# The causal limit of stick breaking attention: a maximum and a product on VectorE in place of a matmul that adds to the scores

## The chip, the cores and the metric

The kernel runs on one core of one Trainium2 chip. The time is device microseconds of one execution of the whole program. A core has five engines with a queue each: TensorE (matmul, with its weight loads shown apart), VectorE, ScalarE, GpSimd and SyncE, which only issues transfers here. TensorE's clock has two levels, 1.2 and 2.4 GHz; the profile gives the granted clock as a share of the higher one.

## The reference

The program computes two transformer blocks on 1024 tokens of width 1024 in float32. The change lies in one stage of the first block, stick breaking attention with 8 heads of width 64:

```python
def stick_breaking_attention(q, k, v):        # per block of 128 queries, keys 0 to end
    z = jnp.einsum('bhqd,bhkd->bhqk', qb, kb).astype(jnp.float32) * scale
    mask = s_pos[None, :] < t_pos[:, None]
    log_one_minus = jnp.where(mask, jax.nn.log_sigmoid(-z), 0.0)
    shifted = jnp.concatenate(
        [log_one_minus[..., 1:], jnp.zeros_like(log_one_minus[..., :1])], axis=-1)
    between = lax.cumsum(shifted, axis=3, reverse=True)
    weights = jnp.where(mask, jnp.exp(jax.nn.log_sigmoid(z) + between), 0.0)
    outs.append(jnp.einsum('bhqk,bhkd->bhqd', weights.astype(vb.dtype), vb))
```

So the weight of key s for query t is sigmoid(z_ts) times the product of sigmoid(-z_tj) over all keys j between s and t, for s < t, and zero elsewhere. Only the 128x128 block on the diagonal holds both allowed and forbidden pairs; blocks beyond it are never computed.

## The kernel before

`stick_breaking` (from line 1693) runs some 300 us of the program, from about 240 to 542 us of the span. Its work is cut into N = 64 steps: step n is head n // 8 and query tile i = n % 8, with L = 128 (i + 1) keys, so the tiles of a head grow from 128x128 (step 0 of the head) to 128x1024 (step 7). What follows calls a step by its i. Beside the attention, the stage carries one projection (`lin_G`): each step also computes one tile of 128 tokens of one weight chunk, and each head one chunk, to fill TensorE.

No planner orders the work. `unrolled(N, [(lag, stage), ...])` writes each engine's queue out by hand: in turn m, an engine does each of its stages for step m - lag, in the order of the list. Engines meet through semaphores alone. Per step:

- TensorE: `scores` (lag 0, L1834 and L1836), `project_tile` (lag 4, L1867 and L1869), `turn_w`, the transposes of the weights (lag 2, L1844), and `values` (lag 3, L1854). The scores are products of q in two parts with k's high part and then k's low part, in pieces of 512 keys. At their end one more product adds `unit` x `limit`, both 128x128 in bf16, to the diagonal block: unit is the identity, limit is 0 for s < t and -1e30 elsewhere, so both sigmoids of a forbidden pair come out as 1 and 0.
- ScalarE: `sigmoids` writes sigmoid(-z) to sb_rest (L1891) once the scores are there, and sigmoid(z) to sb_wgt (L1894) once `turn_w` of two steps ago has read that buffer; then it copies the transposed weights to sb_wT (L1901, lag 2). In step 5 it also rounds q and k of the next head (L1882, L1883), and once per head the weight chunk (L405).
- VectorE: `stage_lin` (lag 4: L1937 and L1939, both from PSUM), `products` (a backward running product over sb_rest, L1919, then sb_wgt times sb_rest shifted by one key, L1922), and `output` (lag 3, the copy of the values to sb_o, L1930). In this order in every step. The scan works in place.
- GpSimd: the low parts, by a subtraction of rounded from full values: q (L1790) and k (L1794) of the next head, once ScalarE has rounded them, and the weight chunk in four pieces (L1814).

Three waits matter: `stage_lin` waits for the projection of its step; `values` of a step waits for `output` of the step before it (`reached(pe, out, n)`), since both use one PSUM bank; `output` sits behind `products` of a step three later in VectorE's queue. Buffers sb_rest, sb_wgt and sb_wT are double.

Of the kernel before, what the change touches and what calls it, by code (L numbers as in the profile page):

```python
# [19 lines left out]
BF = mybir.dt.bfloat16  # L20
# [4 lines left out]
P = 128  # L25
# [5 lines left out]
NEG = -1e30  # L31
# [1661 lines left out]
def stick_breaking(k, qkT, v, mix, lin, lin_dst, mod_stored):  # L1693
# [9 lines left out]
    with ExitStack() as c:  # L1703
        sem = lambda n: k.sem("sb_" + n)
        q = k.sb(c, "sb_q", [P, S])
        q_split = [k.sb(c, f"sb_q_split{s}", [P, S], R) for s in range(2)]
        kk, k_lo = [], []
        for s in range(2):
# [7 lines left out]
        wgt = [k.sb(c, f"sb_wgt{s}", [P, S]) for s in range(2)]  # L1716
        wT = [k.sb(c, f"sb_wT{s}", [P, NT, P]) for s in range(2)]
        o = [k.over(f"sb_o{s}", [P, NT, HD], F, k.w_hl_offset(s, 0, KT * LW)) for s in range(2)]
        limit = k.sb(c, "sb_limit", [P, P], BF)
        unit = k.sb(c, "sb_unit", [P, P], BF)  # L1720
        stage = [k.over(f"sb_stage{s}", [P, NT // 2, LW], F, k.w_hl_offset(s, 1, KT * LW)) for s in range(2)]
        lin_stored = [sem(f"lin_stored{s}") for s in range(2)]
        hi_lo = sem("hi_lo")
# [1 line left out]
        loaded = [sem(f"loaded{s}") for s in range(2)]  # L1725
        v_in = [sem(f"v_in{s}") for s in range(2)]
        stored = [sem(f"stored{s}") for s in range(2)]
        z_done, rest_done, beta_done, scanned, w_done, turned, wT_done, pv, out, his, los = (
            sem(n) for n in ("z", "rest", "beta", "scanned", "w", "turned", "wT", "pv", "out", "his", "los"))
        N = SB_HEADS * NT  # L1730
# [4 lines left out]
        with nc.Block() as block:  # L1735
# [46 lines left out]
            @block.gpsimd  # L1782
            def _(pool):
                def split_qk(n):
                    h, s = n // NT, n // NT % 2
                    if n % NT == 0:
                        pool.wait_ge(his, 2 * h + 1)
                        if h:
                            pool.wait_ge(*lin.at("w_ready", slot(h - 1), (h - 1) // 2 + 1))
                        pool.tensor_tensor(q_split[s][HD:P, :], q[HD:P, :], q_split[s][HD:P, :].bitcast(F),  # L1790
                                           ALU.subtract).then_inc(los, 1)
                        pool.wait_ge(los, 2 * h + 1)
                        pool.wait_ge(his, 2 * h + 2)
                        pool.tensor_tensor(k_lo[s][:, :], kk[s][:, :], k_hi[s][:, :].bitcast(F),  # L1794
                                           ALU.subtract).then_inc(los, 1)
                pool.memset(limit[:, :], 0.0).then_inc(made, 1)
                pool.memset(unit[:, :], 0.0).then_inc(made, 1)
                for s in range(2):
                    pool.memset(rest[s][:, :], 1.0).then_inc(made, 1)
                pool.wait_ge(made, 4)  # L1800
                pool.affine_select(out=limit[:, :], in_=limit[:, :], compare_op=ALU.is_gt, fill=NEG, base=0,
                                   pattern=[[-1, P]], channel_multiplier=1).then_inc(made, 1)
                pool.affine_select(out=unit[:, :], in_=unit[:, :], compare_op=ALU.not_equal, fill=1.0, base=0,
                                   pattern=[[-1, P]], channel_multiplier=1).then_inc(made, 1)
                pool.wait_ge(made, 6)
                split_qk(0)

                def split_lo(n):
                    part, sl, j = n % NT, slot(n // NT), n // NT // 2
                    if part < 4:  # L1810
                        if part == 0:
                            pool.wait_ge(*lin.at("w_hi_done", sl, j + 1))
                        cols = slice(part * KT * LW // 4, (part + 1) * KT * LW // 4)
                        lo = pool.tensor_tensor(k.w_lo[sl][:, cols], k.w_raw[sl][:, cols],  # L1814
                                                k.w_hi[sl][:, cols].bitcast(F), ALU.subtract)
                        if part == 3:
                            lo.then_inc(k.wsem["w_ready"][sl], 1)
                unrolled(N, [(0, split_lo), (-3, lambda n: split_qk(n) if n else None)])

            @block.tensor  # L1820
            def _(pe):
                pe.wait_ge(made, 6)

                def scores(n):
                    h, i = n // NT, n % NT
                    s, L = h % 2, (i + 1) * P
                    if i == 0:
                        pe.wait_ge(los, 2 * h + 2)
                        pe.wait_ge(loaded[s], 64 * (h // 2 + 1))
                    reached(pe, beta_done, n - 1)  # L1830
                    for a in range(0, L, 512):
                        b = min(L, a + 512)
                        for part in (k_hi, k_lo):
                            pe.matmul(zs(n, a, b), q_split[s][:, i * P:(i + 1) * P], part[s][:, a:b],  # L1834
                                      start=part is k_hi, stop=part is k_lo and b < L)
                    pe.matmul(zs(n, L - P, L), unit[:, :], limit[:, :], start=False, stop=True)\  # L1836
                      .then_inc(z_done, 1)

                def turn_w(n):
                    i = n % NT  # L1840
# [71 lines left out]
            @block.vector  # L1912
            def _(dve):
                def products(n):
                    L = (n % NT + 1) * P
                    w, left = wgt[n % 2], rest[n % 2]
                    dve.wait_ge(rest_done, n + 1)
                    back = left[:, 0:L][:, ::-1]
                    dve.tensor_tensor_scan(back, back, back, 1.0, ALU.mult, ALU.min).then_inc(scanned, 1)  # L1919
                    dve.wait_ge(scanned, n + 1)  # L1920
                    dve.wait_ge(beta_done, n + 1)
                    dve.tensor_tensor(w[:, 0:L], w[:, 0:L], left[:, 1:L + 1], ALU.mult).then_inc(w_done, 1)  # L1922

                def output(n):
                    h, i = n // NT, n % NT
                    s = h % 2
                    dve.wait_ge(pv, n + 1)
                    if i == 0:
                        reached(dve, stored[s], 16 * (h // 2))
                    dve.tensor_copy(o[s][:, i, :], k.bank[6][:, 0:HD]).then_inc(out, 1)  # L1930

                def stage_lin(n):
                    tile, sl, half = n % NT, slot(n // NT), n % NT // 4
                    dve.wait_ge(*lin.at("lin_mm", sl, NT * (n // NT // 2) + tile + 1))
                    if tile % 4 == 0:
                        reached(dve, lin_stored[half], 16 * (n // NT))
                    dve.tensor_copy(stage[half][:, tile % 4, :], k.bank[7][:, LW:2 * LW]).then_inc(hi_lo, 1)  # L1937
                    dve.wait_ge(hi_lo, n + 1)
                    dve.tensor_tensor(stage[half][:, tile % 4, :], k.bank[7][:, 0:LW], stage[half][:, tile % 4, :],  # L1939
                                      ALU.add).then_inc(k.wsem["lin_evac"][sl], 1)  # L1940
                unrolled(N, [(LATE, stage_lin), (0, products), (3, output)])


# [1637 lines left out]
```

## Time and profile before

| | us |
|---|---|
| three executions | 3300.24, 3302.2, 3306.65 (median 3302.2) |
| the profiled execution | 3302.0 |
| its span | 3300.3 |
| busy in the span: TensorE / weight loads | 2938.9 / 2526.1 |
| busy in the span: VectorE / ScalarE / GpSimd | 1851.4 / 1027.9 / 908.1 |
| busy from 243 to 540 us (297 us): TensorE / weight loads | 284.81 / 270.99 |
| busy from 243 to 540 us: VectorE / ScalarE / GpSimd | 205.94 / 138.72 / 88.43 |
| mean granted clock, whole span / 243 to 540 us | 0.943 / 0.95 |

The span is what the profiler saw; the time of an execution has a little around it. Busy times of engines overlap. The start of a matmul is recorded, its end is modelled, so the distance from one start to the next tells more than its duration. "Idle before" is the time in which an engine had nothing running ahead of an instruction, with the instruction that ended it.

### The profile page before, as it was taken

The page shows a single profiled execution, that of the slowest core. Times are in us where ns is not written, and L with a number is a line of the kernel's source. Part 1 is how long each engine was busy: PE and PEld are TensorE (multiplying, and loading weights), DVE is VectorE, ACT ScalarE, POOL GpSimd, SP SyncE. Part 2 cuts the span into 40 slices and gives each one's busy share as a digit, 9 for nine tenths or more (in the row PEclk, how much of TensorE's full clock was granted, in tenths as well). Part 3 has the DMA queues.
Part 4 walks back from the last instruction along what each step waited for, and adds up shares of the span by engine and source line. Part 5 has one row for each costly group of instructions (what it writes and reads, how often), then busy time and mean ns, then how long its engine had stood idle before and what let it go on. Part 6 is the DMA issues. An engine that isn't in the chain of part 4 may idle for free. (4 is left out here: it accounts for less than half of the span.)

```text
span 3300.3 us, 40638 instructions
## 1 busy us (share of the span) xinstructions
PE 2938.9 (89%) x15957; PEld 2526.1 (77%) x15957; DVE 1851.4 (56%) x2924; ACT 1027.9 (31%) x1466; POOL 908.1 (28%) x304
## 2 busy tenths in 40 slices
PE   4969998799999999979677678889999899999996
PEld 3869897687888888867556676789779688888885
DVE  7617764665454545562589877865336533333336
ACT  5424544222222222231456455633222111111111
POOL 1212331113233233340122512211121233333333
PEclk9989998799999999989788789999999999999998
DMA  6733333401111111101223322230102111111111
GB/s 225 264 103 72 72 76 125 164 16 72 40 50 46 56 51 38 64 26 62 67 83 124 92 63 60 63 116 28 43 20 71 64 51 41 48 51 51 51 51 51
DMA packets 112339, 240.06 MB, mean 73 GB/s; under 512 B 53524, under 2 KB 72471, under 8 KB 99015
## 3 DMA queue, kind: packets, MB, share of 16 engines
q1 hardware_dynamic: 107175, 220.70, 20.6%
q10 hardware_dynamic: 4320, 14.29, 1.3%
q0 software_dynamic: 704, 3.15, 0.3%
q8 instruction: 95, 1.56, 0.2%
q14 instruction: 45, 0.37, 0.0%
HBM read 202.58 MB, written 38.67 MB: 73 GB/s over the span
## 5 line engine op out<-in xcount | busy, mean ns | idle before, releaser
L1020 PE MATMUL psum<-h_hi,w_hl 128*128 128x512 f32 x2432 | 751.3, 390 | 16.8 <-DVE ffn_relu L1597 12.8
L1009 POOL TENSOR_TENSOR w_hl<-w_raw,w_hl 128x2048 fp32r<-128x2048 f32 x65 | 324.0, 4984 | 862.9 <-ACT w_hl L1003 862.9
L1020 PEld LDWEIGHTS psum<-h_hi,w_hl 128*128 128x128 f32 x2432 | 456.7, 188 | 113.7 <-issue 18.4
L1037 PE MATMUL psum<-w_hl,ffn_a_hi 128*128 128x512 f32 x1600 | 494.1, 390 | 6.5 <-DVE residual L1360 6.5
L1020 PE MATMUL psum<-h_lo,w_hl 128*128 128x512 f32 x1216 | 473.8, 390 | 0.0
L450 PE MATMUL psum<-w_hl,h_hi 128*128 128x256 f32 (+1 forms) x1920 | 353.8, 287 | 29.9 <-POOL w_hl L413 15.1
L1037 PEld LDWEIGHTS psum<-w_hl,ffn_a_hi 128*128 128x128 f32 x1600 | 301.3, 188 | 69.5 <-DVE residual L1360 6.9
L1003 ACT ACTIVATE w_hl<-w_raw 128x2048 fp32r<-128x2048 f32 x65 | 124.6, 1916 | 692.4 <-PE psum L1037 355.0
L413 POOL TENSOR_TENSOR w_hl<-w_raw,w_hl 128x2048 fp32r<-128x2048 f32 (+1 forms) x39 | 181.8, 4662 | 552.6 <-ACT w_hl L405 552.6
L450 PEld LDWEIGHTS psum<-w_hl,h_hi 128*128 128x128 f32 x1920 | 305.3, 196 | 31.7 <-issue 16.0
L1037 PE MATMUL psum<-w_hl,ffn_a_lo 128*128 128x512 f32 x800 | 311.9, 390 | 0.0
L450 PE MATMUL psum<-h_hi,w_hl 128*128 128x512 f32 (+1 forms) x864 | 254.8, 380 | 39.9 <-POOL h_lo L2855 19.8
L450 PE MATMUL psum<-w_hl,h_lo 128*128 128x256 f32 (+1 forms) x960 | 274.5, 286 | 0.0
L1360 DVE TENSOR_TENSOR residual<-residual,psum 128x512 f32<-128x512 f32 x176 | 120.2, 687 | 274.7 <-PE psum L1037 274.6
L1020 PEld LDWEIGHTS psum<-h_lo,w_hl 128*128 128x128 f32 x1216 | 228.7, 188 | 47.8
L1606 DVE TENSOR_TENSOR residual<-residual,psum 128x512 f32<-128x512 f32 x256 | 172.7, 685 | 132.3 <-PE psum L1037 132.2
L450 PEld LDWEIGHTS psum<-h_hi,w_hl 128*128 128x128 f32 x864 | 160.3, 192 | 71.0 <-POOL h_lo L2855 20.2
L1597 DVE TENSOR_SCALAR ffn_relu<-psum,ffn_b_up 128x512 f32<-128x512 f32 x64 | 46.5, 748 | 284.6 <-POOL ffn_a_lo L1571 158.3
L450 PEld LDWEIGHTS psum<-w_hl,h_lo 128*128 128x128 f32 x960 | 187.9, 196 | 0.0
L1347 DVE SCALAR_TENSOR_TENSOR ffn_u<-ffn_raw,ffn_conv,ffn_u 128x1024 f32<-128x1024 f32 x88 | 181.0, 2118 | 0.0
L1037 PEld LDWEIGHTS psum<-w_hl,ffn_a_lo 128*128 128x128 f32 x800 | 150.6, 188 | 31.4
L450 PE MATMUL psum<-h_lo,w_hl 128*128 128x512 f32 (+1 forms) x432 | 163.0, 377 | 0.0
(375 smaller groups left out, 5078.7 us busy)
## 6 DMA issues: line engine op xcount, KB each, us to landing
w_raw<-in_w_up SPq DMA_DIRECT2D x38, 1024.0 KB, 4.8
w_raw<-in_w_down SPq DMA_DIRECT2D x27, 1024.0 KB, 4.9
ada_w<-in_w_ada ACTq DMA_DIRECT2D x26, 512.0 KB, 4.6
w_raw<-in_w_in_T SPq DMA_DIRECT2D x12, 1024.0 KB, 7.0
ada_w<-in_w_ada SPq DMA_DIRECT2D x22, 512.0 KB, 5.3
w_raw<-in_xa_wkv SPq DMA_DIRECT2D x8, 1024.0 KB, 5.4
w_raw<-in_w_in_G SPq DMA_DIRECT2D x8, 648.0 KB, 5.4
p1G<-sb_stage SPq DMA_DIRECT2D x16, 324.0 KB, 3.6
```

Source lines behind the costliest of these rows:

```text
L413: pool.tensor_tensor(self.k.w_lo[s][:, 0:n], self.k.w_raw[s][:, 0:n], self.k.w_hi[s][:, 0:n].bitcast(F), ALU.subtract)\
L450: mm = pe.matmul(out, lhs, rhs, start=t == 0 and p == 0, stop=t == KT - 1 and p == 2)
L1003: act.activation(self.k.w_hi[s][:, :], self.k.w_raw[s][:, :], ACT.Copy)\
L1009: pool.tensor_tensor(self.k.w_lo[s][:, :], self.k.w_raw[s][:, :], self.k.w_hi[s][:, :].bitcast(F), ALU.subtract).then_inc(self.k.wsem["w_r ...
L1020: m = pe.matmul(k.bank[b][:, :], w[:, t * CW + f * P:t * CW + (f + 1) * P], h[:, t, half * 512:half * 512 + 512], start=t == 0 and w is w_ ...
L1037: m = pe.matmul(k.bank[4 + out % 4][:, :], a[f][:, tile * P:(tile + 1) * P], w[:, f * D + half * 512:f * D + half * 512 + 512], start=f == ...
L1347: dve.scalar_tensor_tensor(out=u[s][:, v, :], in0=raw[s][:, v, j:j + S], scalar=co, in1=u[s][:, v, :], op0=ALU.mult, op1=ALU.add)\
L1360: dve.tensor_tensor(k.x[:, tile, cols], k.x[:, tile, cols], k.bank[4 + o % 4][:, :], ALU.add)\
L1597: dve.tensor_scalar(r[:, b % 2, (b // 2) * 512:(b // 2) * 512 + 512], k.bank[b][:, :], bu[:, ds(2 * g + b % 2, 1)], 0.0, ALU.add, ALU.max) ...
L1606: dve.tensor_tensor(xt, xt, k.bank[4 + o % 4][:, :], ALU.add).then_inc(dn_out, 1)
```

## The change

The matmul with the limit goes. The constants `limit` and `unit` are replaced by `later` (1 for s >= t, 0 elsewhere) and `sooner` (1 for s < t, 0 elsewhere), both 128x128 in float32. In each step VectorE takes the maximum of `later` and the diagonal block of sb_rest before the scan, and multiplies the diagonal block of sb_wgt by `sooner` before the large product. Two semaphores order this. The wait for the constants moves from TensorE to VectorE; ScalarE keeps its own.

```diff
-        limit = k.sb(c, "sb_limit", [P, P], BF)
-        unit = k.sb(c, "sb_unit", [P, P], BF)
+        later = k.sb(c, "sb_later", [P, P])
+        sooner = k.sb(c, "sb_sooner", [P, P])
...
+        limited, weighed = sem("limited"), sem("weighed")
...
-                pool.memset(limit[:, :], 0.0).then_inc(made, 1)
-                pool.memset(unit[:, :], 0.0).then_inc(made, 1)
+                pool.memset(later[:, :], 0.0).then_inc(made, 1)
+                pool.memset(sooner[:, :], 1.0).then_inc(made, 1)
...
-                pool.affine_select(out=limit[:, :], in_=limit[:, :], compare_op=ALU.is_gt, fill=NEG, base=0,
+                pool.affine_select(out=later[:, :], in_=later[:, :], compare_op=ALU.is_gt, fill=1.0, base=0,
                                    pattern=[[-1, P]], channel_multiplier=1).then_inc(made, 1)
-                pool.affine_select(out=unit[:, :], in_=unit[:, :], compare_op=ALU.not_equal, fill=1.0, base=0,
+                pool.affine_select(out=sooner[:, :], in_=sooner[:, :], compare_op=ALU.is_gt, fill=0.0, base=0,
                                    pattern=[[-1, P]], channel_multiplier=1).then_inc(made, 1)
...
-                pe.wait_ge(made, 6)
-
                 def scores(n):
...
                         for part in (k_hi, k_lo):
-                            pe.matmul(zs(n, a, b), q_split[s][:, i * P:(i + 1) * P], part[s][:, a:b],
-                                      start=part is k_hi, stop=part is k_lo and b < L)
-                    pe.matmul(zs(n, L - P, L), unit[:, :], limit[:, :], start=False, stop=True)\
-                      .then_inc(z_done, 1)
+                            mm = pe.matmul(zs(n, a, b), q_split[s][:, i * P:(i + 1) * P], part[s][:, a:b],
+                                           start=part is k_hi, stop=part is k_lo)
+                    mm.then_inc(z_done, 1)
...
                     dve.wait_ge(rest_done, n + 1)
+                    dve.tensor_tensor(left[:, L - P:L], left[:, L - P:L], later[:, :], ALU.max).then_inc(limited, 1)
+                    dve.wait_ge(limited, n + 1)
                     back = left[:, 0:L][:, ::-1]
                     dve.tensor_tensor_scan(back, back, back, 1.0, ALU.mult, ALU.min).then_inc(scanned, 1)
+                    dve.wait_ge(beta_done, n + 1)
+                    dve.tensor_tensor(w[:, L - P:L], w[:, L - P:L], sooner[:, :], ALU.mult).then_inc(weighed, 1)
                     dve.wait_ge(scanned, n + 1)
-                    dve.wait_ge(beta_done, n + 1)
+                    dve.wait_ge(weighed, n + 1)
                     dve.tensor_tensor(w[:, 0:L], w[:, 0:L], left[:, 1:L + 1], ALU.mult).then_inc(w_done, 1)
...
+                dve.wait_ge(made, 6)
                 unrolled(N, [(LATE, stage_lin), (0, products), (3, output)])
```

## Rows read from the trace of the kernel before

**Rows 1.** Head by head: stretch, busy of PE, PEld, DVE, ACT, POOL, PEclk, DMA.

```profile
268.73:304.77 36.04, 34.29 (x270) 32.56 (x270) 26.13 (x41) 17.71 (x28) 12.35 (x6) 1.00 0.34 82
...
414.53:452.82 38.29, 36.74 (x271) 35.22 (x270) 25.29 (x41) 17.43 (x27) 11.97 (x6) 0.92 0.32 75
```

**Rows 2.** Waits of the whole stage: us in total, times, longest us.

```profile
PE psum L1854 <- DVE sb_o L1930: 11.7, 11, 1.6
...
DVE sb_stage L1937 <- PE psum L1869: 73.6, 51, 3.0
...
PEld psum L1836 <- issue: 7.4, 32, 0.5
...
PE psum L1844 <- DVE sb_wgt L1922: 0.5, 2, 0.3
```

**Rows 3.** TensorE's timeline at three head changes: start, duration, engine, line, operation [idle before].

```profile
374.51 0.82 PE L1844 MATMUL psum<-ident,sb_wgt 128*128 128x128 f32 x6
...
376.88 1.30 PE L1854 MATMUL psum<-w_raw,sb_wT 128*128 128x64 f32 x10 [1.55 <-DVE sb_o L1930]
...
381.56 0.52 PE L1854 MATMUL psum<-w_raw,sb_wT 128*128 128x64 f32 x3 [0.19 <-DVE sb_o L1930]
...
412.93 0.29 PE L1854 MATMUL psum<-w_raw,sb_wT 128*128 128x64 f32 x1 [1.55 <-DVE sb_o L1930]
...
420.43 0.33 PE L1854 MATMUL psum<-w_raw,sb_wT 128*128 128x64 f32 x2
```

**Rows 4.** VectorE's timeline, steps 5 to 7 of head 3, same columns.

```profile
366.03 0.33 DVE L1937 COPY sb_stage<-psum 128x162 f32<-128x162 f32 x1 [0.58 <-PE psum L1869]
...
366.64 1.75 DVE L1919 TENSOR_TENSOR_SCAN sb_rest<-sb_rest 128x768 f32<-128x768 f32 x1
...
368.42 0.96 DVE L1922 TENSOR_TENSOR sb_wgt<-sb_wgt,sb_rest 128x768 f32<-128x768 f32 x1
...
369.29 0.22 DVE L1930 COPY sb_o<-psum 128x64 f32<-128x64 f32 x1
...
370.76 2.73 DVE L1919 TENSOR_TENSOR_SCAN sb_rest<-sb_rest 128x896 f32<-128x896 f32 x1
...
373.52 3.08 DVE L1922 TENSOR_TENSOR sb_wgt<-sb_wgt,sb_rest 128x896 f32<-128x896 f32 x1
...
377.25 2.28 DVE L1919 TENSOR_TENSOR_SCAN sb_rest<-sb_rest 128x1024 f32<-128x1024 f32 x1
...
379.56 1.72 DVE L1922 TENSOR_TENSOR sb_wgt<-sb_wgt,sb_rest 128x1024 f32<-128x1024 f32 x1
```

**Rows 5.** GpSimd's timeline, the same stretch.

```profile
368.79 2.81 POOL L1790 TENSOR_TENSOR sb_q_split<-sb_q,sb_q_split 64x1024 fp32r<-64x1024 f32 x1 [22.17 <-ACT sb_q_split L1882]
...
371.69 3.97 POOL L1794 TENSOR_TENSOR sb_k_lo<-sb_k,sb_k_hi 128x1024 fp32r<-128x1024 f32 x1
...
378.34 5.55 POOL L1814 TENSOR_TENSOR w_hl<-w_raw,w_hl 128x324 fp32r<-128x324 f32 x4 [2.69 <-ACT w_hl L405]
```

**Rows 6.** GpSimd's timeline at the start of the stage.

```profile
237.31 2.35 POOL L1790 TENSOR_TENSOR sb_q_split<-sb_q,sb_q_split 64x1024 fp32r<-64x1024 f32 x1 [5.36 <-ACT sb_q_split L1882]
```

**Rows 7.** TensorE's timeline around one limit product.

```profile
367.58 0.34 PE L1834 MATMUL psum<-sb_k_lo,sb_q_split 128*128 128x384 f32 x1
...
367.76 0.23 PE L1836 MATMUL psum<-sb_limit,sb_unit 128*128 128x128 bf16 x1
...
367.80 0.40 PE L1867 MATMUL psum<-w_hl,h_hi 128*128 128x324 f32 x1
```

**Rows 8.** Two lines asked for: durations ns min/median/max of all their instructions.

```profile
L1922 DVE TENSOR_TENSOR sb_wgt<-sb_wgt,sb_rest x64: 292/802/3084, 244.0 to 527.3; 128x128 f32<-128x128 f32 x8, 128x256 f32<-128x256 f32 x8, 128x384 f32<-128x384 f32 x8, 128x512 f32<-128x512 f32 x8
...
L1814 POOL TENSOR_TENSOR w_hl<-w_raw,w_hl x32: 867/1031/1863, 242.0 to 493.7; 128x324 fp32r<-128x324 f32 x32
```

**Rows 9.** Two projections, columns as in rows 1.

```profile
378.29:380.44 2.15, 2.15 (x19) 2.15 (x18) 2.12 (x2) 0.28 (x1) 2.10 (x2) 1.00 1.01 292
...
415.09:419.02 3.93, 3.93 (x18) 3.93 (x18) 2.33 (x3) 0.28 (x1) 3.93 (x4) 0.50 0.60 193
```

## The prediction

> **What bounds the kernel now.** I first cut the stage by heads, from the start of one head's first score product to the next [rows 1]. Two of the six periods are 36.04 us at clock 1.00, the other four are longer at a lower mean clock, up to 38.29. In the 36.04 us TensorE is busy for 34.29 and VectorE for 26.13. So TensorE sets the pace, and the mean says that VectorE has 10 us free. The mean misleads: 1.75 us of TensorE's idle time per head has to be found. The list of waits [rows 2] says that TensorE's value products (L1854) waited 11 times, 11.7 us in all, for VectorE's copy to sb_o (L1930), while VectorE waited 73.6 us for the projection (L1869). VectorE has slack in some steps and is late in others. TensorE's timeline shows where: 1.55 us ahead of the value products of step 7, and 0.19 us ahead of those of step 0 of the next head [rows 3]. Nothing else in a full-clock head stops TensorE.
>
> Next I read why VectorE is late there, on VectorE's and GpSimd's timelines of the same 20 us [rows 4, 5]. The scan takes 1.75 us for 768 columns and 2.28 for 1024, so 2.01 would fit 896, but it took 2.73; the product took 0.29 for 128 [rows 8] and 0.96 for 768, so 1.09 would fit 896 and 1.22 fit 1024, but they took 3.08 and 1.72. GpSimd's q and k subtractions took 2.81 and 3.97 there against 2.35 for q's before VectorE had begun [rows 6] (k's is as wide, and I take 2.34). The sums agree with taking turns: the scan issued at 370.76 ends 1.9 us after q's subtraction (ended 371.60), k's subtraction then loses 1.63, and the product issued at 373.52 ends 0.94 us after k's ended at 375.66. So VectorE's work on two SBUF operands and GpSimd's subtractions exclude each other, and whoever waits gets the next turn. The copies and sums from PSUM (L1937, L1939) keep 0.33 us beside them.
> The Trainium skill (SBUF — State Buffer, § SBUF: two separate sides) states it as a lock held for the whole instruction, against a VectorE operation with two SBUF inputs; this speaks against a change that adds two such operations per step. Priced by their own durations alone they give the first rival below; priced by the lock, the forecast. By that rule, the trace agrees.
>
> **The change, part by part.**
> *Limit product removed (L1836), 64 times.* From its start to the next product is 0.04 us (367.76 to 367.80); from k_lo's product to the projection 0.22, of which its own 384 columns at 2.4 GHz are 0.16, which leaves 0.06 [rows 7]. I take 0.05 us each. The upper bound is 7.4 us of weight-load idle time "issue" before it in 32 cases [rows 2], 0.12 us each over 64. In the steps where TensorE waits for VectorE nothing is gained; some 43 steps are left (1 to 5 of seven heads, all of the last): a gain of 2.2 us, between 1.7 and 5.2.
> *Added:* maximum (sb_later) ahead of the scan and product (sb_sooner) after it, 64 times each, 128x128. The shortest product, on a 128x128 tile, took 292 ns [rows 8]. An operation waiting for the one before starts 0.03 us after its end (scan to product, 368.39 to 368.42), one that does not starts 0.08 before it (copy at 369.29, product end 369.38) [rows 4]. So the maximum costs 0.32, the second product 0.21: 0.53 us per step. Queued behind them on VectorE are the large product, the output copy and the next step's staging; TensorE waits for the copy (L1854), ScalarE for the large product.
> *Moved:* the wait for the constants goes from TensorE, which has its score products behind it, to VectorE, which has its staging and scans behind it; the constants, now float32, are still two memsets and two selects of GpSimd, which then idles 5.36 us for q's rounding [rows 6], and no score or sigmoid exists before this: nothing. ScalarE's first sigmoid may start 0.2 us sooner; VectorE starts on staging, not on it: nothing.
> *Steps 0 to 4:* VectorE idles before the next staging; the least of these times is 0.58 us (366.03, [rows 4]), their mean 73.6/51 = 1.4 us [rows 2]. It covers 0.53 in each.
> *Steps 5 to 0, walked on the full-clock head of rows 3 to 5.* In step 5 staging starts at 366.03, maximum 366.64, scan 366.96 to 368.71, small product to 368.92. Q's subtraction asks at 368.79, so it gets the next turn: to 371.27. The large product follows, to 372.2, copy to 372.3, and the values of step 6 start at 372.45, some 2 us late. Step 6: staging 372.2; k's subtraction has the turn from 372.15 to 374.5, then maximum to 374.8, scan to 376.8, small product to 377.0, large one to 378.15, copy to 378.3, values of step 7 at 378.4 instead of 376.88: **1.5 us late**. If q's subtraction comes after step 5's product, the waits change places but their sum is the same within 0.1.
> Step 7: TensorE, held up at step 6, ends its projection at 376.45 instead of 374.51; GpSimd's weight pieces started 3.83 us after this (378.34), so now at 380.3. Maximum from 378.75, scan 379.07 to 381.35. If a piece (0.87 us alone, rows 8) gets in before the small product and another before the large one, the values of step 0 start at 384.8; if the small product keeps the turn, at 383.9. Before: 381.56. So **2.3 to 3.25 us per head**, middle 2.8, at full clock.
> *The clock.* The 16 products of a projection took 2.15 us at clock 1.00 and 3.93 at 0.50, that is at 2.4 and at 1.2 GHz [rows 9], the slow one right after a stall of 1.55 us (412.93, [rows 3]). From the stalled values of step 7 to those of step 0 took 7.50 us there (412.93 to 420.43), against 4.68 [rows 3]. Three of the seven head changes lose a projection's clock like this; the same stall of 1.55 us left it at 1.00 in the others. With three stalls of 1 to 2 us in place of one I expect the clock to fall in three of the four heads that keep it now. There step 0's values come at 378.4 + 7.5 = 385.9, 4.3 us later than now. In the three that lose it now TensorE hides VectorE's step 7, and 1.55 us stay.
> *Start.* In head 0, TensorE already waits for VectorE's product (L1844) [rows 2], so the first steps' additions show: two steps of 0.53 and half a GpSimd piece, 1.5 us (0.5 to 3).
> *The sum:* 4 heads x (3/4 x 4.3 + 1/4 x 2.8) = 15.7; 3 x 1.55 = 4.7; start 1.5; product -2.2. Together +19.7. The profiled execution took 3302.0 us (span 3300.3 and 1.7 around it), the median of the three runs is 3302.2. 3302.0 + 19.7 = 3321.7, rounded to **3322**. Nothing after the stage is touched; it moves as a whole.
>
> **The rivals.**
> *A: VectorE pays only durations.* GpSimd's subtractions fall where the small operations are not hurt. Then steps 6 and 7 cost 0.53 each and another 0.2 of displaced idle time: 1.3 us x 7 = 9, start 1, product -2.2: 3310. For it: the total of GpSimd work is unchanged. Against: in steps 5 to 7 every turn is already contested [rows 4, 5].
> *B: slower still.* The three stalls keep the clock low twice per head. A second slow projection costs 1.8 us more [rows 9]: 7 x (4.3 + 1.8) = 43, less what is lost now in three heads (5.9, see C), start 1.5, product -2: 3339. For it: the stalls at steps 6, 7 and 0 lie 4 to 6 us apart. Against: a slow TensorE waits less, which ends the stalls.
> *C: faster.* The stall of step 7 goes with the low clock in three heads, at up to 2.25 us each (38.29 less 36.04, [rows 1]), 5.9 in all as an estimate. If the operations go one to a gap, the stall grows by 0.53 per head and its later place keeps the clock full: 3.7 + 0.5 - 5.9 - 5.2 (upper bound of the product) = -6.9: 3295. It decides from the point where the clock stays at 1.0 through all head changes. Against: more idle time of TensorE has gone with a lower clock in this trace, not a higher.
> *D: no change that can be told.* The additions sit in the stall as in A and the limit product gives its upper bound: 3302 + 9 + 0.5 - 5.2 = 3306.
>
> **How the numbers follow.** Forecast 0.55 (3313 to 3332), A 0.18, B 0.12, C 0.04, D 0.11. A measurement of this kernel tells 0.2%, 6.6 us. Faster is C: 0.04. Same is D and the lower part of A (below 3308.6): 0.15. Slower 0.81. The range leaves out C, half of D and half of B: 3305 to 3339.
>
> **What would show it.** In the profile after: L1836 gone and score to projection 0.17 us; two groups of 64 on VectorE, with a mean above 0.4 us because some waited for a turn, and a bare minimum of 0.29; values of L1854 waiting for L1930 now also at step 6, with 11.7 us grown to over 30; head periods of 38.3 to 40.5 us instead of 36.04; low clock at nearly every head change; q's subtraction at about 2.4 us since it starts first. I am wrong if the small operations show 0.29 us throughout (A), if idle time of L1854 does not grow, or if the clock stays at 1.0.

## The result: 0.13% slower, where 0.6% was forecast

The changed kernel took 3307.32 us in the median of 20 executions, the kernel before 3304.59 in 20 on the same chip; the ratio is 1.0013 with a 95% interval of 1.0007 to 1.0019, so 2 to 6 us more. The direction was right and the range held the time, but the forecast was +20 us and the measured difference is +4.3. Most of the expected loss did not come. One execution of the changed kernel, in its second series, took 9669.9 us and is left out of every number here; why is not known.

The page of the changed kernel (span 3302.3 us) shows the work moved as described: VectorE has 40 us more than the 1851.4 of before and 128 instructions more, TensorE 64 products fewer.

```profile
PE 2940.6 (89%) x15893; PEld 2530.5 (77%) x15893; DVE 1891.3 (57%) x3052; ACT 1027.1 (31%) x1466; POOL 892.4 (27%) x304
```

Two heads of the changed kernel, in the columns of [rows 1]:

```profile
309.84:346.89 37.05, 35.10 (x262) 33.81 (x262) 31.27 (x57) 17.59 (x28) 9.92 (x6) 0.95 0.35 80
...
457.75:497.68 39.93, 36.73 (x262) 35.45 (x262) 31.40 (x57) 16.31 (x26) 10.61 (x6) 0.91 0.32 74
```

Of its six head periods four are 36.77 to 37.05 us and two 39.9; the latter are called the dear heads below. The kernel before had 36.04 to 38.29, 36.73 in the mean; here the mean is 37.96. The stage (to the end of the last staging) ended at 547.5 us against 541.5. The two waits of [rows 2] in the stage, with their new line numbers (L1852 waits for L1932, L1939 for L1867):

```profile
PE psum L1852 <- DVE sb_o L1932: 16.9, 16, 1.7
...
DVE sb_stage L1939 <- PE psum L1867: 39.0, 24, 3.1
```

TensorE waited 16.9 us for VectorE's output copy instead of 11.7, not the 30 that I expected, and VectorE's waiting for the projection halved. The two new operations, grouped by form (count, busy us, mean ns of one, idle before):

```profile
L1916 DVE TENSOR_TENSOR sb_rest<-sb_rest,sb_later 128x128 f32<-128x128 f32 x64 | 28.5, 445 | 19.7 <-ACT sb_rest L1889 19.7
...
L1921 DVE TENSOR_TENSOR sb_wgt<-sb_wgt,sb_sooner 128x128 f32<-128x128 f32 x64 | 22.1, 345 | 0.0
```

VectorE's timeline in steps 5 to 7 of head 3, the lines that answer to [rows 4], and GpSimd's for [rows 5]:

```profile
373.08 0.27 DVE L1921 TENSOR_TENSOR sb_wgt<-sb_wgt,sb_sooner 128x128 f32<-128x128 f32 x1
...
373.45 2.98 DVE L1924 TENSOR_TENSOR sb_wgt<-sb_wgt,sb_rest 128x768 f32<-128x768 f32 x1
...
377.08 1.73 DVE L1916 TENSOR_TENSOR sb_rest<-sb_rest,sb_later 128x128 f32<-128x128 f32 x1
...
378.85 2.02 DVE L1919 TENSOR_TENSOR_SCAN sb_rest<-sb_rest 128x896 f32<-128x896 f32 x1
...
385.94 1.23 DVE L1924 TENSOR_TENSOR sb_wgt<-sb_wgt,sb_rest 128x1024 f32<-128x1024 f32 x1
```

```profile
373.25 2.37 POOL L1791 TENSOR_TENSOR sb_q_split<-sb_q,sb_q_split 64x1024 fp32r<-64x1024 f32 x1 [19.62 <-ACT sb_q_split L1880]
...
375.70 2.96 POOL L1795 TENSOR_TENSOR sb_k_lo<-sb_k,sb_k_hi 128x1024 fp32r<-128x1024 f32 x1
...
386.08 2.74 POOL L1815 TENSOR_TENSOR w_hl<-w_raw,w_hl 128x324 fp32r<-128x324 f32 x2 [7.42 <-ACT w_hl L405]
```

The large product of step 5 now takes 2.98 us instead of 0.96: q's subtraction (asked at 373.25) got its turn between the small product (ended 373.35) and it. The maximum of step 6 waited for k's subtraction (1.73 us), the scan over 896 columns then ran beside no subtraction (2.02 instead of 2.73), and the weight pieces came at 386.08, after step 7's large product had been issued (1.23 instead of 1.72). TensorE's timeline of the same head: three rows of step 6's scores and projection for [rows 7], and the value products in the turn of step 6 (they belong to the tile three steps earlier, by their lag of 3; start, duration, line, idle before):

```profile
372.04 0.34 PE L1833 MATMUL psum<-sb_k_lo,sb_q_split 128*128 128x384 f32 x1
...
372.22 0.31 PE L1865 MATMUL psum<-w_hl,h_hi 128*128 128x324 f32 x1
...
372.37 0.24 PE L1867 MATMUL psum<-w_hl,h_lo 128*128 128x162 f32 x1
...
376.72 0.52 PE L1852 MATMUL psum<-w_raw,sb_wT 128*128 128x64 f32 x3 [1.72 <-DVE sb_o L1932]
```

A new stall of 1.72 us stands at step 6. After it the clock fell, here in step 7. The rows below are step 7's scores and projection together, its projection alone (3.22 us at a mean clock of 0.61), and the start of its value products, which waited for nothing:

```profile
377.61:382.25 4.64, 4.64 (x23) 4.35 (x23) 4.50 (x5) 1.03 (x1) 1.05 (x1) 0.63 0.00 0
...
379.03:382.25 3.22, 3.22 (x18) 3.22 (x17) 3.12 (x4) 1.03 (x1) 0.00 (x0) 0.61 0.00 0
...
382.90 0.33 PE L1852 MATMUL psum<-w_raw,sb_wT 128*128 128x64 f32 x2
```

### The profile page after: what moved, and what is told of

Read it like the earlier page. It is cut to its first block and busy times, and to the rows that moved or that the text cites. A ratio compares the mean times of both kernels' runs of the same rounds, so it can differ in the third digit from the quotient of the medians.

```text
span 3302.3 us, 40638 instructions
## 1 busy us (share of the span) xinstructions
PE 2940.6 (89%) x15893; PEld 2530.5 (77%) x15893; DVE 1891.3 (57%) x3052; ACT 1027.1 (31%) x1466; POOL 892.4 (27%) x304
```

## The experiments

Theory after the result: (1) VectorE's work on two SBUF operands and GpSimd's subtractions take turns, and this, not the 0.53 us of the additions, sets what the change costs; (2) the limit product was dearer than I had it; (3) where the clock falls matters more than that it falls. Rivals are named with each run. Each ratio is against the kernel before on the same chip, medians in us. Periods are from the start of one head's first score product to the next.

### The limit product alone

```diff
...
-                    pe.matmul(zs(n, L - P, L), unit[:, :], limit[:, :], start=False, stop=True)\
-                      .then_inc(z_done, 1)
+                    mm.then_inc(z_done, 1)
```

> Before with the limit product L1836 left out and nothing in its place (the causal limit inside the diagonal blocks is not computed). Theory: the product costs TensorE 0.13 us per step, 0.04 until the next product starts and 0.09 that the next products start later, in every step in which TensorE does not wait. So score products plus projection take 2.60 us in step 3 instead of 2.74, a full-clock head 35.3 to 35.5 us instead of 36.04, the program 5 to 8 us less. Rival (the term of my prediction, 0.05 us): 2.69 us in step 3, a head 35.8 us, the program 2 to 3 us less.

Measured: 3297.13, ratio 0.9973 (0.9961 to 0.9984), 9 us less. Scores plus projection of step 3 take 2.60 us instead of 2.74, and a head at full clock:

```profile
305.19:340.65 35.46, 33.37 (x262) 32.42 (x262) 26.27 (x41) 17.69 (x28) 12.61 (x6) 1.00 0.35 83
```

35.46 us, as the theory has it; four of the six periods hold some low clock, at 36.5 to 36.6. The stage ends 6.7 us sooner than in the first profile of before and 3.2 sooner than in the second (below). The product is worth 0.13 us a step. The rows of [rows 7] show what I missed. Before, the first projection product stood 0.24 us ahead of the second (367.80 to 368.04, the next row of that timeline); now it is 0.15 (372.22 to 372.37). So the bf16 product cost 0.04 us until the next start and 0.09 after it.

### The additions alone

```diff
+                    dve.tensor_tensor(left[:, L - P:L], left[:, L - P:L], later[:, :], ALU.max).then_inc(limited, 1)
...
+                    dve.tensor_tensor(w[:, L - P:L], w[:, L - P:L], sooner[:, :], ALU.mult).then_inc(weighed, 1)
...
                     pe.matmul(zs(n, L - P, L), unit[:, :], limit[:, :], start=False, stop=True)\
                       .then_inc(z_done, 1)
```

> Before with the maximum and the small product added on VectorE and the limit product kept (the result stays the reference's). Theory: the additions alone cost what the change costs plus what the limit product gives back: head periods 37.5 to 37.8 us against 37.05 in the changed kernel, the program 9 to 12 us above before. Rival (limit product worth 0.05 us a step): 6 to 7 us above before. My prediction's price for the additions was 22 us.

Measured: 3311.27, ratio 1.0022 (1.0012 to 1.0033), 7 us more. Its stage ended 8.1 us later than in the first profile of before.

```profile
308.22:345.89 37.67, 35.93 (x270) 33.79 (x270) 31.33 (x57) 17.59 (x28) 9.91 (x6) 0.95 0.33 78
```

Four periods are 37.67 to 37.75, 0.63 above the changed kernel's 37.05, which is five unstalled steps at 0.13. The total came out below what I gave the theory and within its interval also where the rival stood, so this run alone doesn't decide between them; the periods do. What it settles is the price of the additions: 7 to 8 us, a third of the 22 that my sum had. The two parts do not add up to the whole: 9 us less and 7 us more would make the changed kernel 2 us faster, and it is 4 slower. The intervals of the two (5 to 13 us less, 4 to 11 more) leave room for most of this difference. The rest can come from where the clock falls: of the six periods one is dear here (38.99) and two are in the changed kernel.

### GpSimd's subtractions taken away, with and without the change

```diff
-                        pool.tensor_tensor(k_lo[s][:, :], kk[s][:, :], k_hi[s][:, :].bitcast(F),
-                                           ALU.subtract).then_inc(los, 1)
+                        pool.memset(k_lo[s][:, :].bitcast(F), 0.0).then_inc(los, 1)
```

and the same for q.

> Before with GpSimd's two subtractions for q's and k's low parts replaced by memsets to zero (the low parts of q and k are left out). Theory (turns for the second SBUF port): the scan over 896 columns falls from 2.73 to 2.01 us and its product from 3.08 to 1.09, the stall of step 7 (1.55 us) and that of step 0 (0.19) go, the clock stays at 1.00, a head takes 34.3 us, the program 15 to 19 us less. Rival (the stall has another cause than the turns): the stall stays over 1 us and the program within 5 us.

> The changed kernel with the same memsets in place of the subtractions (the low parts of q and k are left out). Theory: without the contested turns the additions fit into VectorE's idle time and only the gain of the removed product is left, a head of 33.3 to 33.8 us against 34.3 in the same edit of before, the program 3 to 8 us below that. Rival (the additions cost 0.53 us in each of the late steps whatever GpSimd does): the program at or above the same edit of before.

Measured: 3280.39, ratio 0.9925 (0.9911 to 0.9938), and with the change 3272.45, ratio 0.9903 (0.9888 to 0.9918). One head of each, and the two groups of the first that were slow in [rows 4]:

```profile
330.71:364.52 33.81, 33.81 (x270) 32.50 (x270) 23.04 (x41) 17.60 (x28) 5.88 (x6) 1.00 0.36 87
```

```profile
L1917 DVE TENSOR_TENSOR_SCAN sb_rest<-sb_rest 128x896 f32<-128x896 f32 x8 | 16.1, 2015 | 0.0
...
L1920 DVE TENSOR_TENSOR sb_wgt<-sb_wgt,sb_rest 128x896 f32<-128x896 f32 x8 | 8.7, 1092 | 0.3
```

```profile
331.41:364.93 33.52, 33.30 (x262) 32.41 (x262) 27.82 (x57) 17.59 (x28) 6.51 (x6) 1.00 0.36 88
```

With nothing to take turns with, the scan over 896 columns takes 2.02 us and its product 1.09, TensorE is busy for the whole head, and the clock is 1.00. So the stall of step 7 came from the turns with GpSimd's subtractions. A memset of 0.95 us that ran beside a large product (357.09 to 358.04 beside 356.74 to 357.70) stretched neither (0.96 and 0.95 us, as elsewhere in this run); it reads nothing from SBUF. The Trainium skill (SBUF — State Buffer, § SBUF: two separate sides) limits the lock to GpSimd operations that read SBUF when VectorE has two SBUF inputs, and this trace agrees. In this setting the change is no loss: a head is 33.52 us against 33.81. It gains 0.28 us, not the 1.0 of eight steps at 0.13, since the additions still reach TensorE in step 0, where it comes to the values 0.39 us later than in the other kernel (a stall of 0.22 us among it), and a little in step 4. In the stage the two end within 0.2 us of each other; the further 8 us between their medians lie outside it (see the last section).

### The subtractions cut in two, the later halves moved

```diff
-                        pool.tensor_tensor(k_lo[s][:, :], kk[s][:, :], k_hi[s][:, :].bitcast(F),
-                                           ALU.subtract).then_inc(los, 1)
+                        pool.tensor_tensor(k_lo[s][:, 0:512], kk[s][:, 0:512], k_hi[s][:, 0:512].bitcast(F),
+                                           ALU.subtract).then_inc(los, 1)
...
+                def split_rest(n):
+                    h, s = n // NT, n // NT % 2
+                    if n % NT == 4:
+                        pool.wait_ge(*lin.at("w_ready", slot(h), h // 2 + 1))
+                        pool.tensor_tensor(q_split[s][HD:P, 512:S], q[HD:P, 512:S],
+                                           q_split[s][HD:P, 512:S].bitcast(F), ALU.subtract).then_inc(rests, 1)
+                        pool.wait_ge(rests, 2 * h + 1)
+                        pool.tensor_tensor(k_lo[s][:, 512:S], kk[s][:, 512:S], k_hi[s][:, 512:S].bitcast(F),
+                                           ALU.subtract).then_inc(rests, 1)
...
+                    if i == 4:
+                        pe.wait_ge(rests, 2 * h + 2)
```

GpSimd's queue has `split_rest` right behind the weight pieces, so it runs in the first steps of the head.

> Before with GpSimd's q and k subtractions of the next head cut in two: columns 0 to 511 in their old place (steps 5 and 6), columns 512 to 1023 after the weight pieces, in the first steps of the head that needs them from step 4 on; everything is computed. Theory (turns): the contested time in steps 5 and 6 falls from 4.7 to 2.35 us, scan and product of 896 columns together from 5.8 to about 4 us, the stall of step 7 goes, a head takes 33.8 to 34.3 us, the program 18 to 25 us below before. Rival (only the amount of GpSimd work counts, not when it comes): the stall of step 7 stays above 1 us and the program within 5 us of before.

> The changed kernel with the same cut. Theory: q's first half still gets its turn during the small product of step 5, so the large product waits 1.2 us and step 6 stalls by 0.5 to 1 us, steps 7 and 0 by 0.2 to 1.3; a head takes 34.5 to 35.5 us, the program 5 to 12 us above before with the cut, and still 10 us or more below before. Rival (the additions are free once the contest is halved): at or below before with the cut, by the gain of the removed product, some 8 us.

Measured: 3281.38, ratio 0.9934 (0.9921 to 0.9947); with the change 3291.19, ratio 0.9964 (0.9951 to 0.9978).

```profile
333.42:367.30 33.88, 33.88 (x270) 32.52 (x270) 24.89 (x41) 17.59 (x28) 9.73 (x8) 1.00 0.37 88
```

```profile
338.31:373.58 35.27, 33.72 (x262) 32.49 (x262) 30.27 (x57) 17.59 (x29) 10.28 (x8) 1.00 0.35 84
```

```profile
PE psum L1865 <- DVE sb_o L1945: 11.2, 15, 0.9
```

All six periods of either are alike to 0.02 us, at full clock. Without the change a head is 33.88 us, with it 35.27, with a stall of 0.64 at step 6 and 0.92 at step 0 (the row of waits is of the changed kernel with the cut). What the two theories gave for the head and the program holds; of the stalls, the one at step 7 did not come. Here, where the clock plays no part, the change costs 1.39 us per head and 10 us in all: the price of the additions against halved turns. And the kernel before with this cut, **22 us faster than the kernel before, is the fastest complete kernel of this study.**

### Filling the stall of the kernel before

```diff
+                    if i == 4:
+                        pe.wait_ge(beta_done, n + 3)
+                        for _ in range(6):
+                            pe.matmul(zs(n, 0, 512), q_split[s][:, 0:P], k_hi[s][:, 0:512],
+                                      start=True, stop=True)
                     reached(pe, out, n)
```

Value products have a lag of 3, so those of tile 4 (`i == 4`) are the ones that TensorE issues in the turn of step 7.

> Before with six needless products of 512 columns (some 1.3 us) issued ahead of TensorE's wait in step 7, into a score bank that is free then. Theory (the idle time of 1.55 us is what lowers the clock in three of seven heads): the projection of step 0 takes 2.15 us in all heads, every period is 36.0 to 36.4 us, the stage ends 3 to 6 us sooner. Rival (the clock falls for another reason): one to three slow projections of over 3 us stay and the time is before's.

Measured: 3292.90, ratio 0.9967 (0.9956 to 0.9979).

```profile
340.18:376.25 36.07, 35.72 (x277) 33.59 (x276) 26.16 (x41) 17.72 (x28) 12.38 (x6) 1.00 0.35 82
```

All six periods are 36.06 or 36.07 at clock 1.00. So the idle 1.55 us is what lowered the clock. The stage ended at 535.7 us, 5.8 sooner than in the first profile of before and 2.4 sooner than in the second; the six periods together are 3.3 to 4.0 us shorter. Where the rest of the 11 us comes from is not shown.

### Only the maximum

```diff
-                    dve.tensor_tensor(w[:, L - P:L], w[:, L - P:L], sooner[:, :], ALU.mult).then_inc(weighed, 1)
```

> The changed kernel without the small product (the weights of the diagonal block are not limited, the rest is). Theory: the small product is what lets q's subtraction in ahead of the large product of step 5. Without it the large product of 768 columns takes 0.96 us again instead of 2.98, the stall of step 6 goes, that of step 7 grows to 2.3 to 2.8 us, and the clock falls after step 7, in the projection of step 0, where nothing hides it: heads of 36.5 us at full clock and over 38 where it falls, so the program is no faster than with the product, within 4 us of the changed kernel. Rival (each operation costs its own 0.2 to 0.3 us in each late step): the stall of step 6 stays, only shorter, and the program is 2 to 5 us below the changed kernel.

Measured: 3300.95, ratio 0.9994 (0.9986 to 1.0003), 6 to 7 us below the changed kernel, and the stall of step 6 stayed (1.72 us in every head). My theory of what lets q's subtraction in was wrong. At the end of step 5's scan, GpSimd's and VectorE's rows:

```profile
333.00 2.38 POOL L1791 TENSOR_TENSOR sb_q_split<-sb_q,sb_q_split 64x1024 fp32r<-64x1024 f32 x1 [19.47 <-ACT sb_q_split L1880]
...
333.02 3.18 DVE L1922 TENSOR_TENSOR sb_wgt<-sb_wgt,sb_rest 128x768 f32<-128x768 f32 x1
```

The maximum alone moves the scan back by 0.32 us and the product is issued 0.02 us after q's subtraction has asked. In [rows 4, 5] it was issued 0.37 us before. So the maximum alone is enough to turn the order; the small product alone was not run. The six periods are 36.2 to 37.3 us. The rival had the right sign, and the small product costs its share in each late step, more than the 2 to 5 us given; the stall of step 6 did not get shorter as it said. So the operations' own time counts beside the turns, and theory (1) holds in part.

### The changed kernel with the clock kept up in step 7

The same filling products, seven of them, with `if i == 3`, so ahead of the wait in the turn of step 6.

> The changed kernel with seven needless products of 512 columns (some 1.5 us) ahead of TensorE's wait in step 6. Theory: the low clock that follows the stall of step 6 costs the changed kernel nothing, since it lies in step 7, where TensorE would wait for VectorE anyway, and it makes GpSimd's weight pieces late enough to miss VectorE's step 7. With the clock kept up there, step 7 stalls by 1.0 us and step 0 by 1.5 us in every head: heads of 37.8 us and more, up to 39.9 where the clock then falls in steps 0 and 1, and the program 3 to 15 us above the changed kernel in spite of a higher clock in step 7. Rival (each fall of the clock costs what its slow products cost): the program 5 us or more below the changed kernel.

Measured: 3318.51, ratio 1.0047 (1.0034 to 1.0059), 10 us above the changed kernel in its second series below. Two heads, and the projection of step 7 in the first:

```profile
308.49:348.10 39.61, 36.98 (x269) 35.26 (x269) 31.20 (x57) 17.59 (x28) 10.71 (x6) 0.96 0.31 74
...
348.10:386.18 38.08, 35.43 (x269) 33.72 (x269) 31.22 (x57) 17.60 (x28) 10.74 (x6) 1.00 0.33 77
...
343.01:345.08 2.07, 2.07 (x18) 2.07 (x17) 2.04 (x2) 1.03 (x1) 0.12 (x1) 1.00 0.00 0
```

Values of steps 7 and 0 at one head change:

```profile
307.38 0.85 PE L1857 MATMUL psum<-w_raw,sb_wT 128*128 128x64 f32 x6 [1.10 <-DVE sb_o L1937]
...
313.27 0.41 PE L1857 MATMUL psum<-w_raw,sb_wT 128*128 128x64 f32 x2 [1.49 <-DVE sb_o L1937]
```

With step 7 at clock 1.00 (2.07 us for the projection), a full-clock head takes 38.04 to 38.08 us, a microsecond more than the 37.05 with the low clock. The stalls of 1.10 and 1.49 us, which the slow step had covered or removed, are back. The filling itself held nothing up: the values of step 6 start 0.27 us after the copy that they wait for (0.36 in the changed kernel). This is the strongest evidence that the low clock in step 7 costs the changed kernel nothing.

### The other order of turns

```diff
-                        act.activation(q_split[s][:, :], q[:, :], ACT.Copy).then_inc(his, 1)
                         act.activation(k_hi[s][:, :], kk[s][:, :], ACT.Copy).then_inc(his, 1)
+                        act.activation(q_split[s][:, :], q[:, :], ACT.Copy).then_inc(his, 1)
...
-                        pool.wait_ge(his, 2 * h + 1)
+                        pool.wait_ge(his, 2 * h + 2)
```

> The changed kernel with ScalarE rounding k before q, so that q's subtraction asks for its turn 1 us later, after VectorE's large product of step 5. Theory: step 6 has no stall then, step 7 one of 2.5 to 3.4 us, the clock falls in the projection of step 0 instead of in step 7, where nothing hides it, and the weight pieces contest VectorE's step 7: heads of 38.5 to 40.5 us, the program 8 to 20 us above the changed kernel, about where my prediction put the change (3322). Rival (the order of the turns does not matter, as in my prediction's walk, and the clock's fall is hidden anyway): within 4 us of the changed kernel.

Measured: 3318.55, ratio 1.0054 (1.0041 to 1.0067). The large product of step 5, q's subtraction, the scan of step 6 and the stalled values of step 7, and two heads:

```profile
339.01 0.96 DVE L1924 TENSOR_TENSOR sb_wgt<-sb_wgt,sb_rest 128x768 f32<-128x768 f32 x1
...
339.75 2.45 POOL L1791 TENSOR_TENSOR sb_q_split<-sb_q,sb_q_split 64x1024 fp32r<-64x1024 f32 x1 [25.15 <-ACT sb_q_split L1881]
...
342.39 4.15 DVE L1919 TENSOR_TENSOR_SCAN sb_rest<-sb_rest 128x896 f32<-128x896 f32 x1
...
348.20 0.37 PE L1852 MATMUL psum<-w_raw,sb_wT 128*128 128x64 f32 x1 [3.10 <-DVE sb_o L1932]
```

```profile
310.37:350.25 39.88, 36.03 (x262) 34.95 (x262) 32.50 (x57) 17.69 (x27) 11.21 (x8) 0.93 0.34 79
...
350.25:388.91 38.66, 35.55 (x263) 34.67 (x262) 30.86 (x57) 17.69 (x27) 9.36 (x6) 0.94 0.31 71
```

The large product goes first (0.96 us), step 6 has no stall, and the scan waits instead (4.15 us). Step 7 stalls by 3.10 us, the clock falls in the projection of step 0 (3.7 to 3.9 us in all seven head changes), and heads take 38.6 to 40.0. With its order of turns changed, this is the course of the clock that my sum had priced, and it lands 10 us above the changed kernel.

### Both kernels once more

> The changed kernel once more, for a second profile. Theory: four or more of the six periods at 37.05 us, the others at 39 to 40, the stall of 1.7 us ahead of the values of step 6 in every head. Rival (the place of the low clock is chance): slow projections in other steps, periods scattered between 36 and 40 us.

> The kernel before once more, for a second profile. Theory: a stall of 1.55 us at step 7 of every head, a slow projection of step 0 in two to five of seven heads, periods of 36.04 us where it stays away and 36.3 to 38.5 where it does not. Rival (the low clock has nothing to do with the stall): slow projections elsewhere in the stage.

Measured: 3308.44 in 11 executions, ratio 1.0013 (1.0004 to 1.0022), and 3303.65, ratio 1.0007 (0.9998 to 1.0016). Two heads of each:

```profile
309.60:346.64 37.04, 35.09 (x262) 33.80 (x262) 31.29 (x57) 17.57 (x28) 9.93 (x6) 0.95 0.34 80
...
269.69:309.60 39.91, 36.70 (x262) 35.41 (x262) 31.40 (x57) 16.29 (x26) 10.62 (x6) 0.91 0.31 74
```

```profile
342.86:378.90 36.04, 34.29 (x270) 32.56 (x270) 26.14 (x41) 17.70 (x28) 12.35 (x6) 1.00 0.36 82
...
305.68:342.86 37.18, 35.63 (x271) 34.12 (x270) 26.22 (x41) 17.70 (x28) 12.23 (x6) 0.95 0.34 78
```

The second profile of the changed kernel repeats the first: 39.91, three times 37.03 to 37.05, 36.74, then 38.34; that of before has three periods of 36.04 or 36.05 and three of 37.16 to 37.18. The slow projections are those of step 0 (before) and of step 7, or step 1 in the dear heads (after). The stage ended at 545.6 and 538.1 us, 7.5 apart, where the first pair had 5.9.

## Why the forecast was wrong, step by step

**The diagnosis and the walk at full clock: right.** In the head change of the changed kernel where the clock stayed up through steps 7 and 0, the values of steps 7 and 0 started here:

```profile
456.65 0.52 PE L1852 MATMUL psum<-w_raw,sb_wT 128*128 128x64 f32 x3 [1.04 <-DVE sb_o L1932]
...
462.53 0.63 PE L1852 MATMUL psum<-w_raw,sb_wT 128*128 128x64 f32 x4 [1.48 <-DVE sb_o L1932]
```

Step 6's first score product lies at 445.42 there and at 366.86 in the walked head, 78.56 us apart. So these are 378.09 and 383.97 on the clock of the walk, which had 378.4 and 383.9 to 384.8. The values of step 6 came at 372.26 (forecast 372.45). The turns, q's getting ahead in step 5 and the new stall of step 6 are in the trace as walked; only its cause, the small product, was half the truth, since the maximum is enough. The sizes fit too: a head at full clock costs 2.0 us (38.04 with the stall filled, against 36.04), where 2.8 was forecast without what the limit product gives back, five steps of 0.13 us. At full clock the change costs 2.0 us a head with the whole subtractions in the late steps, 1.39 with half of them and -0.28 with none, so the loss hangs on the turns.

**"The clock": this step failed.** I had a stall of 2 us at step 6 in the walk, and still let the clock fall after step 7, with the price of the slow stretch of before, 4.3 us per head for three heads of four. It fell after the first stall instead, in five of seven head changes. There step 7's scores and projection took 4.64 us (377.61 to 382.25) instead of the 3.08 at full clock (451.71 to 454.79), and this time was nearly free: TensorE would have waited 1.04 us for VectorE at step 7 anyway. Its values started without a wait, 6.18 us after those of step 6, against 5.83 in the full-clock head change. Slow work in front of a wait that ends late costs little or nothing. It did more: GpSimd's weight pieces follow the end of step 7's projection by 3.83 us, as I had it, so they came at 386.08 and missed VectorE's step 7. At full clock they came before its two products:

```profile
458.62 5.29 POOL L1815 TENSOR_TENSOR w_hl<-w_raw,w_hl 128x324 fp32r<-128x324 f32 x4 [5.84 <-ACT w_hl L405]
...
459.53 0.90 DVE L1921 TENSOR_TENSOR sb_wgt<-sb_wgt,sb_sooner 128x128 f32<-128x128 f32 x1
...
460.54 1.71 DVE L1924 TENSOR_TENSOR sb_wgt<-sb_wgt,sb_rest 128x1024 f32<-128x1024 f32 x1
```

The two took 0.27 and 1.23 us in the slow head, 1.1 us less, and the values of step 0 came 10.73 us after those of step 6 instead of 11.71. So the head with a low clock in step 7 is 1 us shorter than the one without, and by these rows it is so through GpSimd. Such a head costs 1.0 us (37.05 against 36.04), or 1.6 without the limit product's gain (37.68 in the run of the additions alone), where I had 2.8 to 4.3. In the other two head changes the clock stayed up until step 1 and fell there; these are the dear heads, and their 3.9 us are near the 4.3 that I had for three heads of four. The two runs that force the course of the forecast, by filling the stall and by turning the order, show that the place of the fall made the difference: each is 10 us dearer. And the falls that before paid for, 0.6 to 0.7 us per head in its mean period, went away in these heads; I had left them in.

**The limit product: sized at 0.05 us a step, 0.13 measured.** Over the 43 unstalled steps of my sum 5.6 us are given back instead of 2.2. I had read the distance to the next product and not the one after.

**The start: right.** The first head change came 1.2 us later (1.5 forecast, within 0.5 to 3).

**The sum with what was measured**, in the first pair of profiles: start 1.2, six periods 37.96 - 36.73 = 1.23 each, 7.4, the last head 2.6 less (before had a slow projection in it, after none): +5.9 us in the stage. In the second pair it is +7.5, and 19.7 was forecast.

**"Nothing after the stage is touched; it moves as a whole": off by 3.9 us**, and by 3.6 in the second pair, the other way than the stage. In the first pair, 3.0 us of this lie in one stretch of 489 products that both kernels share. Before and after, in the columns of [rows 1]:

```profile
1502.60:1621.37 118.77, 91.91 (x489) 79.07 (x487) 32.81 (x87) 22.07 (x47) 13.68 (x6) 0.87 0.25 76
...
1508.00:1623.85 115.85, 89.59 (x489) 77.18 (x487) 32.76 (x87) 21.91 (x47) 13.68 (x6) 0.90 0.25 78
```

It takes 115.7 to 115.9 us at a mean clock of 0.88 to 0.90 in nine of the fourteen profiles and 117.5 to 119.6 at 0.87 in five. The run without the limit product is among the fast ones and the one with the additions alone among the slow ones, so this is not an effect of the change by itself; what decides it is open. The ratio over all executions, +4.3 us, holds both the stage and this. In the two pairs the forecast is thus missed by 8 to 10 us in the heads (the clock), by 3.4 in the limit product and by 3.6 to 3.9 after the stage.

**The rivals.** D had 3306, which is +4.3, the measured difference to the digit, and that is luck: its condition, that the additions sit in idle time and wait for no turn, is not what the trace shows, and some 4 us of the measured sum come from outside the stage. Its term for the limit product (5.2) was near the truth. A had about the right size for a head (1.3 us for the additions; the run with the additions alone has 1.1 in the mean) by the wrong reason, since the maximum does wait: 445 ns in the mean, 282 in the kernel without the subtractions. That the range held the time is owed to the half of D that it took in.

## What to carry to other kernels

When one engine is late, follow the time with every wait that comes after and ask where the clock falls: slow products cost only where nothing else would be waited for. A forecast should try the low clock behind each new stall and not only where it was before; here it fell behind the first one in five of seven head changes. Before adding small operations with two SBUF inputs to VectorE, look at what GpSimd reads in those microseconds: an operation of 0.3 us turned the order here and made a neighbour 2 us longer, and moving the GpSimd work (22 us here) was worth several times the change itself. Price a removed product by two distances, the one to the next product and the one after that.

## What the runs showed of the hardware that I had not expected

- A bf16 product of 128 columns between float32 ones delays the product after it: 0.24 us to the second projection product with it, 0.15 without.
- 1.3 us of needless products in a stall of 1.55 us kept the clock at 1.00 in all six periods of a kernel that otherwise loses it in three of seven head changes, in both profiles, and the program took 11 us less (ratio 0.9967).
- A higher clock can make a kernel slower: 38.08 us per head with step 7 at 1.00, 37.05 with it at 0.61, because GpSimd's weight pieces then meet VectorE's products of step 7.
- Open: code after the stage that is the same in all kernels took from 2754.8 us (changed kernel) to 2766.0 (before without subtractions) between profiles. One stretch of it gives up to 4 us of this, with a mean clock that differs by 0.01 to 0.03 (see above); the rest is not traced to a place. So differences of totals below some 5 us between these kernels are not all of the stage, and the 8 us between the two kernels without subtractions are not explained by it.
